# Order of the two products of each stationary weight block: rounded part first, remainder second

## What is computed

```python
proj = jnp.einsum('bsd,dc->bsc', x, w_in[l])           # 6144 columns; queries and keys are 4096 of them
...
attn_out = jnp.einsum('bsc,cd->bsd', mix, w_out[l])
x = layer_norm(DEEPNORM_ALPHA * x + attn_out, ln1_g[l], ln1_b[l])
hdn = jnp.square(jax.nn.relu(jnp.einsum('bsd,df->bsf', x, w_ff1[l])))   # 8192 columns
ff_out = jnp.einsum('bsf,fd->bsd', hdn, w_ff2[l])
```

## Time and profile before

| | |
|---|---|
| runs | 1092.07 to 1092.74 us, median 1092.44 us |
| profiled execution | 1092.65 us, its span 1090.6 us |
| TensorE busy | 1086.1 us of the span, granted clock 1.0 (full) |
| VectorE / ScalarE busy | 808.7 / 572.0 us |
| DMA | 213.83 MB, mean 196 GB/s |
| matmul records | 5611, as many weight loads |

### The profile page before, as it was taken

How to read it: one execution, slowest core, us unless ns; L and a number is a source line. 1 busy time by engine, 2 the same in 40 slices (tenths; PEclk the granted TensorE clock), 3 DMA queues, 4 the chain that set the end, 5 groups by cost and what they waited for, 6 DMA issues and landing times.

```text
span 1090.6 us, 13914 instructions
## 1 busy us (share of the span) xinstructions
PE 1086.1 (100%) x5611; PEld 922.7 (85%) x5611; DVE 808.7 (74%) x890; ACT 572.0 (52%) x723; POOL 21.9 (2%) x43
## 2 busy tenths in 40 slices
PE   9999999999999999999999999999999999999998
PEld 8888888888888888888888888888888888888886
DVE  6587757767656685667699898666676678889998
ACT  6487757665544524445455454344454455454561
POOL 1000000010000000000000000000000000000000
PEclk9999999999999999999999999999999999999999
DMA  8857655557555835665656556466656755655762
GB/s 292 271 178 221 187 187 155 175 171 251 170 161 167 284 108 159 190 193 174 220 185 230 194 193 231 158 192 190 194 174 202 217 179 194 230 195 191 279 223 78
DMA packets 108047, 213.83 MB, mean 196 GB/s; under 512 B 6784, under 2 KB 38016, under 8 KB 107472
## 3 DMA queue, kind: packets, MB, share of 16 engines
q1 hardware_dynamic: 107216, 209.61, 59.9%
q0 software_dynamic: 624, 3.21, 0.9%
q10 hardware_dynamic: 144, 0.13, 0.0%
HBM read 210.83 MB, written 2.10 MB: 195 GB/s over the span
## 4 chain that ended last, share of the span: by engine, by line
PE 98%; DVE 1%; issue 0%; ACT 0%; DVEq 0%
PE low_ps L789 11%; PE low_ps L628 10%; PE high_ps L789 10%; PE high_ps L808 8%; PE high_ps L809 8%; PE high_ps L807 8%; PE low_ps L522 6%; PE low_ps L526 6%; PE low_ps L524 6%; PE low_ps L794 5%; PE low_ps L633 5%; PE high_ps L794 5%; PE low_ps L809 2%; PE low_ps L808 2%; PE low_ps L807 2%; PE high_ps L569 1%
## 5 line engine op out<-in xcount | busy, mean ns | idle before, releaser
L1293 DVE TENSOR_TENSOR w_lo<-w_raw,w_hi 128x1024 fp32r<-128x1024 f32 x175 | 213.3, 1223 | 128.3 <-ACT w_hi L966 127.0
L966 ACT ACTIVATE w_hi<-w_raw 128x1024 fp32r<-128x1024 f32 x175 | 185.3, 1059 | 186.3 <-PE low_ps L526 67.1
L789 PE MATMUL low_ps<-x1T,w_hi 128*128 128x512 f32 x512 | 176.7, 393 | 0.0
L628 PE MATMUL low_ps<-xT,w_hi 128*128 128x512 f32 x448 | 157.2, 396 | 0.0
L789 PE MATMUL high_ps<-x1T,w_hi 128*128 128x512 f32 x448 | 155.0, 394 | 0.0
L794 PE MATMUL low_ps<-x1T,w_lo 128*128 128x256 f32 x512 | 136.9, 278 | 0.0
L1617 DVE TENSOR_TENSOR w_lo<-w_raw,w_hi 128x1024 fp32r<-128x1024 f32 x72 | 87.1, 1223 | 64.6 <-ACT w_hi L1165 64.6
L633 PE MATMUL low_ps<-xT,w_lo 128*128 128x256 f32 x448 | 124.3, 283 | 0.0
L1165 ACT ACTIVATE w_hi<-w_raw 128x1024 fp32r<-128x1024 f32 x72 | 76.1, 1059 | 88.8 <-PE low_ps L789 43.4
L794 PE MATMUL high_ps<-x1T,w_lo 128*128 128x256 f32 x448 | 119.8, 278 | 0.0
L808 PE MATMUL high_ps<-w_lo,hid 128*128 128x512 f32 x290 | 112.4, 388 | 0.0
(11 more groups left out here) (216 smaller groups left out, 1913.7 us busy)
## 6 DMA issues: line engine op xcount, KB each, us to landing
w_raw<-in_w_ff SPq DMA_DIRECT2D x208, 512.0 KB, 4.4
w_raw<-in_w_in SPq DMA_DIRECT2D x93, 512.0 KB, 4.2
more_raw<-in_w_ff SPq DMA_DIRECT2D x42, 512.0 KB, 5.3
w_raw<-in_w_out SPq DMA_DIRECT2D x32, 512.0 KB, 3.7
x_raw<-in_x_turned SPq DMA_DIRECT2D x8, 256.0 KB, 6.3
y<-in_x SPq DMA_DIRECT2D x8, 256.0 KB, 4.7
side_raw<-in_w_ff SPq DMA_DIRECT2D x4, 512.0 KB, 6.7
w_raw<-in_w_in SPq DMA_DIRECT2D x6, 256.0 KB, 5.0
```

Of the source, the lines that this page charges most:

```text
L628: return pe.matmul(banks[:, b, :], w_hi[:, slot, cols], xT[:, t, :, :].rearrange("p h t -> p (h t)"), start=(t == 0), stop=(t == KT - 1))
L789: return pe.matmul(banks[:, b, :], w_hi[:, slot, cols], x1T[:, t, :, :].rearrange("p h t -> p (h t)"), start=(t == 0), stop=(t == KT - 1))
L966: act.activation(w_hi[:, slot, :], w_raw[:, slot, :], ACT.Copy).then_inc(w_rounded, units)
L1293: dve.tensor_tensor(w_lo[:, slot, :], w_raw[:, slot, :], w_hi[:, slot, :].bitcast(F32), ALU.subtract).then_inc(w_split, units)
```

## The change

In all three functions H now comes before L for every k tile but the last; in the last (t = 15), L comes before H, so that H closes the bank. Before, it was H before L for the first k tile and L before H for all others. The number of products, their operands and their waits stay as they were; the order of instructions on the other engines is the same.

```diff
@@ qk_products
-                if t == 0:
-                    of_hi()
-                    of_lo()
-                else:
+                if t == KT - 1:
                     of_lo()
                     ins = of_hi()
+                else:
+                    of_hi()
+                    ins = of_lo()
             ins.then_inc(w_used, 1)
@@ first_queries
-                        if t == 0:
+                        if t == KT - 1:
+                            of_lo()
+                            ins = of_hi()
+                        else:
                             of_hi()
                             ins = of_lo()
-                        else:
-                            of_lo()
-                            ins = of_hi()
             ins.then_inc(w_used, 1)
```

## The result

| | before | after |
|---|---|---|
| median of the runs | 1092.49 us (6 runs) | 1098.24 us (6 runs, 1098.0 to 1098.68) |
| span of the profiled execution | 1090.6 us | 1096.6 us |
| ratio | | 1.0054, 95% interval 1.0041 to 1.0067 |

A forecast was written before the change was run, and what follows sets the result against it. The prediction took TensorE, through the distances between its products, as the bound. Its terms 0.78 + 4.68 + 0.6 + 0 + 0 gave +6.1 us, so 1098.5 us, with a range of 1092.8 to 1100.3 us.

The forecast's parts named there:

- What bounds the kernel: Whole kernel: TensorE is the bound, so time is the sum of distances between its products; TensorE busy 1086.1 of 1090.6 us.
- Hidden chunks 1 and 7: Hidden layer, two chunks beginning behind 512-column products: both taken to turn slow, 2 x 0.39 = 0.78 us.
- The other 12 quick chunks: Hidden chunks 3 to 6 and 8 to 15: all taken to turn slow, +4.68 us, with 0 as lower bound.
- some slow: Rival for the chunk heads: they settle quick or slow by turns, 0.64 slow; +3.5 us, 1095.9 us, chance 0.18.
- The query groups: Alternating pairs in qk_products: +0.6 us, half the upper bound of 1.1; other bound -2.0 us if all become quick.
- The first queries: 64 pairs in first_queries, slow already: 0 us, or -0.45 us were they to become quick.
- The unit heads: About 180 heads whose wait for weights now stands on an H behind an L: 0 us, bound 1.8 us.
- The rival from the page's rule: All matmul pairs: distance is columns over 2.4 GHz plus 2.5 ns whatever the neighbours; 0 us, 1092.4 us, shared chance 0.16.
- The sum: Whole kernel: 0.78 + 4.68 + 0.6 + 0 + 0 = +6.1 us, giving 1098.5 us.

The follow-up runs named there:

- the head experiment: Against the kernel before, only the first unit of each hidden chunk has H, L, H, L for all four banks; 1095.32 us, ratio 1.0023.
- Their blocks: Against the kernel before, first_queries and qk_products issue H in a row and L in a row, hidden_unit unchanged; 1091.39 us, ratio 0.9986.
- The kernel without any head of a chunk: Against the kernel before, hidden_unit issues H before L for all 16 k tiles, L closing the bank, queries unchanged; 1098.89 us, ratio 1.0057.
- the one with two chunks changed: Against the kernel before, hidden chunks 3 and 10 alone have H, L, H, L in their first unit; those chunks took 22.59 and 22.60 us.

## Why the prediction was right, and where its reasons were not

**What bounds the kernel** held: TensorE is the chain, and the whole difference is in the distances between its products. No new wait of any weight came with it.

**Hidden chunks 1 and 7** were taken as slow, 2 x 0.39 us. They are: 0.38 each. H, L, H, L behind 512-column products goes the slow way at both, as at the one place in the trace before. For chunk 1 this is not the whole reason: in the head experiment it begins the same and comes out quick behind its transposes. The prediction had said that half of its price hangs on that.

**The other 12 quick chunks** were the open term, 0 to 4.68 us, taken at its upper end. They lost 12 x 0.38 = 4.6 us. The value was right, and in part by luck; the reason was too simple. I chose the upper bound "since the order at the head is that of rows 9". The head experiment has that order at the head of all chunks and only half of them are slow. What is true of the changed kernel is that its last unit, H, L, L, H for each bank, is followed by a slow chunk every time, with H, L, H, L at its head. That the two together do so for every one of them was not to be had from the rows before; the rival "some slow" was the price of not knowing it, and it was the outcome of the head experiment (+2.6 us).

**The query groups** were given +0.6 us, half of an upper bound of 1.1. Alone they measured +0.3 us, not to be told from 0, nor from what their untouched code varies by. Two steps behind the term failed. The mean of H was read as a mark of the spacing, and it is none where attention's products interrupt: it rose to 399 ns because the long record behind them moved from an L to an H. And attention's products were said to reset the spacing in any case. That is not so in general: with untouched query code the first three units of the fifth group take 8.33 us before (quick) and 8.45 us in the kernel that changes the hidden layer alone (slow), with the same products ahead of them.

**The first queries**, 0, measured +0.3 us within an interval of 1.0 us to either side, and their spacing stayed slow, as foretold. Their blocks and those of the query groups gave back 1.4 us together.

**The unit heads**, 0, with 1.8 us as the bound. The kernel without any head of a chunk has the wait of every unit's head in the hidden layer on an H behind an L; it lost 0.41 us a chunk, and 64 slow pairs at 7 ns are 0.45. Nothing is left for the waits there.

**The rival from the page's rule** (columns over 2.4 GHz and 2.5 ns) is refuted for this stream: one sequence of products took 22.20 or 22.59 us in chunks of one kernel at full clock. The formula has no term for the neighbours, but its page limits it, which the prediction left out. The Trainium skill, TensorE: Matmul & The Clock Gate, "Back-to-back issue gap", calls it the isolated gap of a single matmul, and says that in a stream of weight loads and matmuls both set the spacing.

**The sum** was +6.1 us, 1098.5 us; measured +5.75 us, 1098.24 us. Of it 5.4 us were the hidden layer's, against 5.46 in the sum.

What stays open is the cause inside the chip. The runs show that the alternation of 512 and 256 columns has two self-sustaining spacings, and that it changes between them at irregular places in the stream (L, L; H, H; 128-column products), or not, depending on a state carried up to there. Which part of TensorE or its memory reads holds that state, no run here tells.

## What to carry to other kernels

Where TensorE is the bound and products of two widths alternate, the order of equal work can count: here up to 2% of that stretch. It was a matter of a state, not of the local order alone: an edit at one place turned later, untouched stretches slow or quick. Read the distance between starts over whole stretches, not the busy share, and look for equal stretches of unequal length. The mean duration of a group of matmuls marked it in the hidden layer and misled in the queries, where other products come between. Runs of one width (blocks of 8 to 16 products) came out between the two here, 5.57 us against 5.55 and 5.65; where stretches are quick already they bring nothing.

## What the runs showed of the hardware that I had not expected

- One and the same sequence of matmuls and weight loads, at full granted clock and with no wait in the list, takes 22.20 or 22.59 us for 64 pairs (0.347 or 0.353 us a pair in its steady part).
- The slow spacing lasted over 576 pairs, 203.5 us, without falling back.
- A chunk with unchanged instructions turned slow because the chunk before it was entered in another way (22.59 instead of 22.20 us).
- The slow spacing has a cycle of three pairs (0.36, 0.35, 0.35 us), and the same head behind a slow chunk led to a slow or a quick one.
- Hidden chunks repeat to 0.01 us across kernels: the slow chunk 2 takes 22.59 us in the kernel before and in the one with two chunks changed (440.81 to 463.40 us there). The query groups, with untouched code, don't: 222.11 to 222.42 us.
